# A ring of eight row tiles for the joint decode, six of them filled during chunk compression

## The reference

```
h = x + W_out( sig(gA) * W_oA(NSA(xn)) + sig(gB) * W_oB(FoX(xn)) ),  xn = RMSNorm(x)
y = h + W_down( gelu(causal_dwconv3(RMSNorm(h) W_up)) * (RMSNorm(h) W_gate) )
```

```
logits = concat([einsum('bthd,bshd->bhts', q, k) * ATTN_SCALE + cq_t - ck ... for each segment])
pr = masked_softmax(logits, mask);  out += einsum('bhts,bshd->bthd', pr, v)
```

## Time and profile before

| | |
|---|---|
| median of 3 runs | 976.39 us (976.25 to 977.01) |
| the profiled execution's own time | 969.93 us |
| its span, first to last instruction | 967.9 us |
| mean granted TensorE clock | 0.958 |
| PE busy | 867.2 us, 90% |
| DVE, ACT, POOL busy | 531.2, 367.1, 152.2 us |
| read from memory | 187.44 MB |
| decode stage, first transpose to first transpose of merge | 364.26 to 596.29 us |

### The profile page before, as it was taken

The page is one execution under the profiler, slowest core; times in us unless marked ns, Lnnn a source line. Parts: engine busy times, 40 slices in busy tenths (PEclk is TensorE's granted clock), DMA queues, the critical chain, the costliest instruction groups (busy, mean ns, idle before and its releaser), DMA issues. The chain is left out here.

```text
span 967.9 us, 18265 instructions
## 1 busy us (share of the span) xinstructions
PE 867.2 (90%) x7225; PEld 711.8 (74%) x7225; DVE 531.2 (55%) x982; ACT 367.1 (38%) x657; POOL 152.2 (16%) x255
## 2 busy tenths in 40 slices
PE   2899538979999999999999976999979999999996
PEld 1788337778988987665665533999669989898984
DVE  5544377863343476673465524555556656566654
ACT  2232455544243433363223412434325444344430
POOL 0000303301112103323333330000001101010100
PEclk9899877999999999999999986999979999999999
DMA  6352196017422349989999997968124553465311
GB/s 210 121 166 76 32 286 233 25 52 170 175 94 88 108 156 373 382 307 380 415 419 414 375 417 213 237 166 300 43 70 153 206 182 130 133 204 184 130 43 58
DMA packets 95963, 191.82 MB, mean 198 GB/s; under 512 B 7418, under 2 KB 74778, under 8 KB 83514
## 3 DMA queue, kind: packets, MB, share of 16 engines
q1 hardware_dynamic: 80060, 87.58, 29.4%
q0 software_dynamic: 14544, 102.90, 27.3%
q10 hardware_dynamic: 1296, 0.45, 0.2%
HBM read 187.44 MB, written 7.64 MB: 202 GB/s over the span
## 5 line engine op out<-in xcount | busy, mean ns | idle before, releaser
L244 PE MATMUL banks<-tokens_turned_high,w_gates_high 128*128 128x288 f32 x320 | 96.9, 303 | 3.7 <-PEq L191 2.3
L1429 PEld LDWEIGHTS banks<-consts_base,stream_rows 128*128 128x128 f32 x672 | 74.4, 143 | 33.3 <-issue 27.3
L246 PE MATMUL banks<-tokens_turned_high,w_gates_low 128*128 128x288 f32 x320 | 96.7, 302 | 0.0
L245 PE MATMUL banks<-tokens_turned_low,w_gates_high 128*128 128x288 f32 x320 | 95.4, 298 | 0.0
L1650 ACT ACTIVATE keys_turned<-banks 128x512 f32<-128x512 f32 x94 | 55.1, 596 | 103.8 <-PE banks L1429 103.7
L1429 PE MATMUL banks<-consts_base,stream_rows 128*128 128x128 f32 x672 | 83.8, 278 | 6.9 <-DMA stream_rows<-in_state_win_k 2.2
L995 PE MATMUL banks<-chunks_turned_high,cmp_w_high 64*128 64x256 f32 (+1 forms) x512 | 76.3, 293 | 5.3 <-DVE cmp_w_low L237 2.7
L995 PE MATMUL banks<-chunks_turned_low,cmp_w_high 64*128 64x256 f32 (+1 forms) x512 | 73.1, 280 | 0.0
L995 PE MATMUL banks<-chunks_turned_high,cmp_w_low 64*128 64x256 f32 (+1 forms) x512 | 72.9, 280 | 0.0
L1631 DVE COPY keys_turned<-banks 128x512 f32<-128x512 f32 x74 | 50.4, 690 | 32.8 <-PE banks L1429 30.0
L244 PEld LDWEIGHTS banks<-tokens_turned_high,w_gates_high 128*128 128x128 f32 x320 | 62.2, 194 | 4.9 <-issue 2.7
(11 more groups left out here) (429 smaller groups left out, 2058.8 us busy)
## 6 DMA issues: line engine op xcount, KB each, us to landing
w_up_gate<-in_w_up SPq DMA_DIRECT2D x12, 1024.0 KB, 7.3
w_up_gate<-in_w_gate SPq DMA_DIRECT2D x12, 1024.0 KB, 9.8
w_down<-in_w_down SPq DMA_DIRECT2D x12, 1024.0 KB, 5.0
w_in_slot<-in_w_in SPq DMA_DIRECT2D x8, 1424.0 KB, 6.2
w_gates<-in_w_in SPq DMA_DIRECT2D x16, 512.0 KB, 5.4
cmp_w<-in_cmp_w_k SPq DMA_DIRECT2D x4, 512.0 KB, 21.2
cmp_w<-in_cmp_w_v SPq DMA_DIRECT2D x4, 512.0 KB, 11.3
stream_rows<-in_state_win_k SPq DMA_DIRECT2D x8, 256.0 KB, 8.7
```

The costliest lines, as they stand in the source:

```text
L244: nc.tensor.matmul(out, lh, rh, start=start, stop=False, **kw)
L245: nc.tensor.matmul(out, lh, rl, start=False, stop=False, **kw)
L246: return nc.tensor.matmul(out, ll, rh, start=False, stop=stop, **kw)
L1429: ins = nc.tensor.transpose(bank(t)[:, q * P:(q + 1) * P], src, ident)
```

## The change

The ring gets eight tiles, and each item waits for item n - 8. Tiles 4 and 5 are placed in the upper half of the bridge, where the raw compression weights lie during compression; POOL fetches items 4 and 5 into them once `w_low` is 8, ahead of items 0 to 3. Tiles 6 and 7 are taken where tiles 4 to 6 stood. To make room, `keys_turned` has two buffers, and a new memory of 16 KB a partition (`shared_16k`) is used in turn by one low part of the input weights with the turned sample tokens, by the low compression weights, by logits and constants of decode, and by the first up and gate weights. Several smaller tiles move into one memory (`decode_side`), over which the merge stage lays its `branch_out` tiles. The first `w_o` load waits for the last use of slot 5 in place of `nacc_taken`, and DVE's last split waits for the last use of slot 4.

```diff
@@ stage_project
-        wl = [c.sb(f"w_in_low{u}", [P, KD, ZC], F32R, ctx=ctx) for u in range(2)]
+        wl = [c.sb("w_in_low0", [P, KD, ZC], F32R, ctx=ctx), c.in_big("w_in_low1", [P, KD, ZC], F32R, 0)]
@@ stage_compress
-        w1l = c.sb("cmp_w1_low", [P, 2 * CS, CH], F32R, ctx=ctx)
+        w1l = c.in_big("cmp_w1_low", [P, 2 * CS, CH], F32R, 0)
...
-            for n in range(4):
-                pool.wait_ge(turned, NSTEP - 4 if n < 2 else NSTEP)
+            pool.wait_ge(w_low, 8)
+            for n in (4, 5, 0, 1, 2, 3):
+                if n < 4:
+                    pool.wait_ge(turned, NSTEP - 4 if n < 2 else NSTEP)
                 gather_decode_rows(c, n)
@@
-DEC_RING = 7
+DEC_RING = 8
@@ stage_decode
-    kbuf = {step: n % 3 for n, step in enumerate(keys)}
+    kbuf = {step: n % 2 for n, step in enumerate(keys)}
+    last_in = lambda r: [item for n, item in enumerate(ring) if n % R == r][-1]
...
-        kT = [c.at(f"keys_turned{u}", [P, 4, 4 * P], F32, u * 4 * 4 * 4 * P) for u in range(3)]
-        FL = c.sb("fox_logits", [P, (SLOTS + 1) * P], ctx=ctx)
-        L = {br: c.sb(f"{br}_logits", [P, W[br]], ctx=ctx) for br in W}
-        pT = [c.at(f"nsa_probs_turned{u}", [P, 4 * P], F32, (12 + u) * 4 * 4 * P) for u in range(2)]
+        kT = [c.at(f"keys_turned{u}", [P, 4, 4 * P], F32, u * 4 * 4 * 4 * P) for u in range(2)]
...
+        FL = place("fox_logits", [P, (SLOTS + 1) * P])
+        L = {"win": place("win_logits", [P, W["win"]]), "cmp": place("cmp_logits", [P, W["cmp"]]), "sel": c.sb("sel_logits", [P, W["sel"]], ctx=ctx)}
+        pT = [c.sb(f"nsa_probs_turned{u}", [P, 4 * P], ctx=ctx) for u in range(2)]
...
-            sp.wait_ge(nacc_taken, 8)
+            release(sp, ring.index(last_in(5)))
             load_wo(c, sp, c.wo, c.wo_in, 0)
...
-            for n in range(4, len(ring)):
+            for n in range(6, len(ring)):
...
-                    if n >= 3:
-                        eng.wait_ge(products, done[keys[n - 3]])
+                    if n >= 2:
+                        eng.wait_ge(products, done[keys[n - 2]])
...
             dve.wait_ge(c.merge_high, 1)
+            release(dve, ring.index(last_in(4)))
             split_low(nc, c.gates_low[:, :, :, :], c.gates[:, :, :, :], c.gates_high[:, :, :, :]).then_inc(c.merge_low, 1)
@@ stage_merge
-        oh = c.sb("branch_out_high", [P, 2, 4, NTOK], F32R, ctx=ctx)
-        ol = c.sb("branch_out_low", [P, 2, 4, NTOK], F32R, ctx=ctx)
+        oh, ol = c.branch_high, c.branch_low
@@ build
+        c.big_at = -(-nc.sbuf_base // 32) * 32
+        c.sb("shared_16k", [P, 4 * KD * P])
...
+            c.stream += [c.at(f"stream_rows{n}", [P, CS * KVW], F32, 4 * (n - 2) * CS * KVW) for n in (4, 5)]
...
-            c.stream += [c.sb(f"stream_rows{n}", [P, CS * KVW], ctx=mid) for n in range(4, DEC_RING)]
+            c.stream += [c.sb(f"stream_rows{n}", [P, CS * KVW], ctx=mid) for n in (6, 7)]
```

More of the change, by code:

```diff
@@ L199, in at, with in_big @@
         return self.nc.alloc_sbuf_tensor_at(name, shape, dt, offset=self.bridge_at + offset)
+    def in_big(self, name, shape, dt, offset):
+        return self.nc.alloc_sbuf_tensor_at(name, shape, dt, offset=self.big_at + offset)
     def constants(self, group, ctx, loaded):
@@ L204, in constants, with constants_in @@
         t = self.sb(f"consts_{group}", [P, src.shape[1]], ctx=ctx)
+        at = 0
+        for name in CONST_GROUPS[group]:
+            self.views[name] = t[:, at:at + self.widths[name]]
+            at += self.widths[name]
+        return lambda e: e.dma_start(t[:, :], src).then_inc(loaded, 16)
+    def constants_in(self, group, place, loaded):
+        src = self.d[f"consts_{group}"]
+        t = place(f"consts_{group}", [P, src.shape[1]])
         at = 0
@@ L1319, in stage_decode, with place @@
     last_turn = lambda step: first[step] + {"keys": 3}.get(step[0], 0) + 1
-    kbuf = {step: n % 3 for n, step in enumerate(keys)}
+    kbuf = {step: n % 2 for n, step in enumerate(keys)}
+    last_in = lambda r: [item for n, item in enumerate(ring) if n % R == r][-1]
     with c.stage() as ctx:
         tiles = [x[:, :].rearrange("p (a e) -> p a e", a=4) for x in c.stream]
-        kT = [c.at(f"keys_turned{u}", [P, 4, 4 * P], F32, u * 4 * 4 * 4 * P) for u in range(3)]
-        FL = c.sb("fox_logits", [P, (SLOTS + 1) * P], ctx=ctx)
-        L = {br: c.sb(f"{br}_logits", [P, W[br]], ctx=ctx) for br in W}
-        pT = [c.at(f"nsa_probs_turned{u}", [P, 4 * P], F32, (12 + u) * 4 * 4 * P) for u in range(2)]
+        kT = [c.at(f"keys_turned{u}", [P, 4, 4 * P], F32, u * 4 * 4 * 4 * P) for u in range(2)]
+        big = [0]
+        def place(name, shape):
+            t = c.in_big(name, shape, F32, big[0])
+            big[0] += -(-4 * int(np.prod(shape[1:])) // 32) * 32
+            assert big[0] <= 16 * KD * P
+            return t
+        FL = place("fox_logits", [P, (SLOTS + 1) * P])
+        L = {"win": place("win_logits", [P, W["win"]]), "cmp": place("cmp_logits", [P, W["cmp"]]), "sel": c.sb("sel_logits", [P, W["sel"]], ctx=ctx)}
+        pT = [c.sb(f"nsa_probs_turned{u}", [P, 4 * P], ctx=ctx) for u in range(2)]
         turned_probs = lambda i: pT[0][:, :] if i == 2 else pT[1][:, (0, P, 0, 2 * P)[i]:(P, 2 * P, 0, 3 * P)[i]] if i < 4 else L["sel"][:, (i - 4) * 4 * P:(i - 3) * 4 * P]
-        acc = [c.at(f"fox_slot_sums{u}", [P, FW], F32, (14 + u) * 4 * FW) for u in range(2)]
+        acc = [c.sb(f"fox_slot_sums{u}", [P, FW], ctx=ctx) for u in range(2)]
         fpT = c.sb("fox_probs_turned", [P, (SLOTS + 1) * P], ctx=ctx)
@@ L1341, in stage_decode @@
         selb = c.sb("block_mask", [P, NSELB], ctx=ctx)
-        selx = c.sb("row_mask_and_shift", [P, P], ctx=ctx)
+        selx = place("row_mask_and_shift", [P, P])
         o = c.sb("nsa_rows_out", [P, KVW], ctx=ctx)
@@ L1354, in stage_decode @@
         nsa_in, select_in = c.sem("nsa_constants_in"), c.sem("select_constants_in")
-        load_nsa, load_select = c.constants("nsa", ctx, nsa_in), c.constants("select", ctx, select_in)
+        load_nsa, load_select = c.constants_in("nsa", place, nsa_in), c.constants("select", ctx, select_in)
         turned, products = c.sem("decode_turned"), c.sem("decode_products")
@@ L2225, in __init__ @@
         self.c = c
-        self.slot = lambda u, ctx: (c.sb(f"w_up_gate{u}", [P, 2, KD, 2 * P], ctx=ctx), c.sb(f"w_down{u}", [P, 2, D], ctx=ctx))
+        self.slot = lambda u, ctx: (c.sb(f"w_up_gate{u}", [P, 2, KD, 2 * P], ctx=ctx) if u else c.in_big("w_up_gate0", [P, 2, KD, 2 * P], F32, 0),
+                                    c.sb(f"w_down{u}", [P, 2, D], ctx=ctx))
         self.w_ug, self.w_dn = [[x] for x in self.slot(0, ctx)]
@@ L2503, in build @@
         c.merge_high, c.merge_low = c.sem("merge_weights_high"), c.sem("merge_weights_low")
+        side = (("nsa_q_decode", [P, DB, NH * DS]), ("fox_q_decode", [P, 4 * 2 * P + 32]), ("nsa_k_turned", [P, 2, 3, P]),
+                ("fox_k_turned", [P, 4, 3, P]), ("cmp_k_turned", [P, ND + PCH]))
+        side_at = -(-nc.sbuf_base // 32) * 32
+        side_sizes = [4 * int(np.prod(shape[1:])) for _, shape in side]
+        c.sb("decode_side", [P, sum(side_sizes) // 4])
+        (c.qb, c.fqb, c.kT, c.fkT, c.kcT) = (nc.alloc_sbuf_tensor_at(name, shape, F32, offset=side_at + sum(side_sizes[:n]))
+                                             for n, (name, shape) in enumerate(side))
+        c.branch_high, c.branch_low = (nc.alloc_sbuf_tensor_at(f"branch_out_{x}", [P, 2, 4, NTOK], F32R, offset=side_at + n * 8 * 4 * NTOK) for n, x in enumerate(("high", "low")))
+        c.big_at = -(-nc.sbuf_base // 32) * 32
+        c.sb("shared_16k", [P, 4 * KD * P])
         c.stored, c.cmp_rows_out = c.sem("results_stored"), c.sem("cmp_rows_stored")
@@ L2512, in build @@
             c.eighth_number = c.sb("eighth_row_as_number", [P, DB], ctx=mid)
[L2513 to L2516, removed]
             c.neglf = c.sb("neg_logf", [P, 3, NH], ctx=mid)
@@ L2519, in build @@
             c.png = c.sb("prompt_branch_gates", [P, QT, 3 * NH], ctx=mid)
-            c.kcT = c.sb("cmp_k_turned", [P, ND + PCH], ctx=mid)
             c.vc = c.sb("cmp_v", [P, DB, KVW], ctx=mid)
             c.stream = [c.sb(f"stream_rows{n}", [P, CS * KVW], ctx=mid) for n in range(4)]
+            c.stream += [c.at(f"stream_rows{n}", [P, CS * KVW], F32, 4 * (n - 2) * CS * KVW) for n in (4, 5)]
             c.fox_in = c.sem("fox_constants_in")
@@ L2532, in build @@
                 with ExitStack() as early:
-                    c.xsT = c.sb("sample_turned", [P, KD, NS], ctx=early)
+                    c.xsT = c.in_big("sample_turned", [P, KD, NS], F32, 4 * KD * ZC)
                     w = [c.at(f"w_in_slot{u}", [P, KD, ZC], F32, u * 4 * KD * ZC) for u in range(2)]
```

## The result

| | median us (range), runs | ratio to before, 95% interval |
|---|---|---|
| before, beside it | 973.90 (968.81 to 977.01), 9 | |
| changed kernel | 968.05 (964.37 to 971.91), 9 | 0.9939 [0.9916, 0.9962] |
| changed, second set | 968.88, 12 | 0.9951 [0.9924, 0.9978] |
| changed, third set | 968.73, 12 | 0.9955 [0.9938, 0.9972] |

The change makes the kernel faster by 4 to 6 us (medians of the three pairs). The forecast was 4.5 us, taken from the 976.39 us of the three runs shown, which are three of the nine in the first row; the time it named, 971.9, and its lower end, 968.8, are both too high. In the sets further down 95 runs of the kernel before had medians of 973.8, 972.2 and 972.4 us.

A forecast was written before the change was run, and what follows sets the result against it. It held that the last tile's landing sets decode's end, after back-to-back transfers with one hole. 2.5 + 2.0 + 0 + 0 = 4.5 us off 976.39 gave 971.9 us, range 968.8 to 976.7.

The forecast's parts named there:

- the level: Whole kernel: the 4.5 us gain subtracted from the shown runs' median, 976.39 us, gives 971.9.
- the term for the hole: Decode, 536 to 544 us: lost transfer time between two late-requested tiles would be regained, 2.0 us.
- rival (b): Tiles fetched before decode count in full, 5.0 us, plus 2.0 for the transfer gap: 969.4 us; chance 0.08.
- (c): Decode's fetch stream gains nothing because the rate falls to 402 GB/s with eight transfers in flight: 976.4 us; chance 0.11.
- Part 1: Decode ring: with eight tiles each fetch is asked for one item earlier, one transfer gained, 2.5 us.
- Part 2: Decode near 540 us: the gap in the transfers closes and the gain reaches the last tile, 2.0 us more.
- Part 3: Before decode: six tiles fetched instead of four count nothing and cost compression nothing, 0 us.
- Part 4: Edits that pay for the memory (two key buffers, moved tiles, later waits, early `w_o`): 0 us, bound 1.3.
- Key copies that wait for products: Decode key steps: seven of 42 delayed by a 1.07 us product step would make the kernel slower.
- `w_o` comes ahead: End of decode: 0.52 MB of this load ahead of the last tiles, bound 1.3 us, taken as 0.
- The tail keeps its length: After decode's last tile: the tail hangs on that tile and its length does not change.
- the 2.5 that it gave as a sign of being wrong: Merge stage: a start less than 2.5 us earlier would show the prediction wrong.

The follow-up runs named there:

- `before_again`: The kernel before, unchanged, timed and profiled once more against itself: 974.22 us, ratio 1.0011.
- the busy tail: Eight and seven tiles, window loads by GpSimd, unread products on TensorE at the end: 965.89 and 968.91 us.
- `ring7_six_early`: Changed kernel with seven tiles in the ring for eight, six still fetched in chunk compression: 973.28 us, 0.9999 of before.
- both experiments: Changed kernel with only four tiles fetched in compression, 967.72 us; and with seven ring tiles, six fetched early, 973.28 us.
- `ring7_windows_pool`: Kernel before, ring of seven, with the window tiles' loads issued by GpSimd in ring order, not SyncE: 969.64 us, 0.9959 of before.
- `after_again`: The changed kernel, unchanged, timed and profiled once more: 968.88 us, 0.9951 of before.
- `ring8_warm`: Changed kernel with unread products on TensorE ahead of the last waits: 967.28 us, 0.9941 of before.

## Why the prediction was half right

**The step that failed is the last one of the sum, the level.** It set the profile's 969.93 us beside the median of three runs, 976.39, and took the 4.5 us from that. The nine runs beside the changed kernel have 973.90, so 2.5 of the 3.9 us by which the forecast missed (971.9 against 968.05) are the level, and 1.4 the effect, which is 5.9 in that pair. Over 107 runs of the kernel before (the 95 and `before_again`'s 12) the median is 972.9 us, with 5% under 969.9 and 5% over 977.5: the three runs stood together in the upper part, the profile at the lower edge. 972.9 - 4.5 = 968.4, and the changed kernel's 33 runs have 968.6. That the effect comes out so close is luck in part, since the term for the hole was small and the terms do not add, as below. The range was built as the effect's alone, from rival (b) to rival (c); it gave the base's own scatter no width at all.

**Part 1, 2.5 us for the eighth tile: right, perhaps a little large.** The bytes at 84 us give one tile, and the last tile stands 2.4 us apart with the windows by GpSimd, 2.0 with the busy tail. In total time it is 3.0 us with the busy tail, and only 0.8 without, where the tails differed.

**Part 2, 2.0 us for the hole: right in kind, and probably too small.** It rests on an execution with one late window item. Two of the three profiles with seven tiles and SyncE's window rows (`before_again`, `ring7_six_early`) have two, and with them the last tile ends its wait at 225.3 and 224.6 us for 222.3. "PE shows no wait on a DMA before 521" was true of only that one of the three. Moving the windows' queue gives the term by itself, 2.0 to 5.9 us in total time, with the short tail of its profile in it. The keys were asked for 3.1 us earlier in the stage (506.36 - 364.26 = 142.1, now 504.66 - 365.61 = 139.1), not the 4.0 that I had from the value step.

**Part 3, early tiles 0: right,** by both experiments. Rival (b) is refuted.

**Part 4, 0: right as far as tried.** The layout with two key buffers, at seven tiles, is at 0.9999 of before, to within 3 us. Key copies that wait for products were one of the prediction's signs of being wrong. The profile after does put two such waits down to products (1.99 us before a copy by DVE at 515.40, 2.70 by ACT at 544.35), but the one at 515.40 is no longer than the copy's wait for its transposes at the same step before, 1.99 us at 513.15, and PE waits for no key copy longer than before (0.7 us). That `w_o` comes ahead (bound 1.3 us) happened and costs nothing that can be measured.

**"The tail keeps its length": wrong, by a cause that I had not looked for.** It is 9.73 and 10.84 us in the two profiles of before, 9.97, 10.84 and 10.84 in three of after, and 8.70 in `ring7_windows_pool`, by the granted clock behind the last waits. It took nothing from the change on average that these five can show, but it is why the two terms do not simply add in the profiles: the window edit alone gets the short tail in its one profile, and the eighth tile on top of it then brought 2.4 us at the tile and 0.3 at the merge stage.

**The sum by steps.** The last tile's wait ends at 222.3 and 225.3 us before, and at 219.2, 217.7 and 218.3 after: means of 223.8 and 218.4, 5.4 us apart. `ring7_windows_pool` stands between them at 220.8: 3.0 us for the window rows and 2.4 for the tile, by single profiles. Outside the stage little changed: its start lies at 364.3 and 366.5 us before and at 365.6, 365.0 and 367.4 after, and from the merge stage's first transpose to the end it is 371.6 and 371.2 us before, and 371.3, 371.6 and 369.5 after, a mean of 0.6 us less. The 5.4 us go with the 4.4 to 5.9 us of the three ratios. The first pair of profiles alone fell short of what the prediction named: the last tile's wait 3.1 us earlier for 4.5, the merge stage 2.9 in the stage's own time and 1.5 in absolute time, which is under the 2.5 that it gave as a sign of being wrong.

## What to carry to other kernels

Where the stream of bytes sets the end, the eighth tile of this ring was worth about one transfer, whatever was fetched before the stage: count the bytes moved by the end of the stretch that the engine sets, and compare. The step from six to seven was worth 14 us, so a transfer for a tile is what it comes to only where the engine hardly stands inside the stream. Before a tile is bought with memory, look at the stream's own stragglers: here moving the window rows to the ring's queue, an edit of a few lines, brought 2.0 to 5.9 us by itself, about as much as the whole change, though one execution in twelve of it took 2163 us for a reason not found. And a median of three runs is a level with its own error; when the profile lies 0.7% beside it, the range has to hold both.

## What was not expected of the hardware

- About half of the scatter between executions goes with TensorE's granted clock: over 107 runs of the kernel before the time and the mean clock (0.949 to 0.966) have a correlation of -0.74, whose square is 0.55, and within the kernels here 0.01 of it goes with 4.2 us. The start of the decode stage lay between 364.3 and 370.4 us in the fourteen profiles; the changed kernel alone had 365.0, 365.6 and 367.4.
- After PE had stood 0.77 and 1.76 us for its last two tiles (`after_again`), the granted clock was 0.50 up to the merge stage 10.84 us later; with unread products in those gaps (`ring8_warm`) it was 0.98. Waits of 1.30 and 1.87 us in `ring7_windows_pool` were not followed by slow steps; what made the difference is open.
- The rate of loads was 411 to 419 GB/s with a ring of six, seven or eight 1.049 MB tiles, from 120 to 172 us of the stage. The Trainium skill, "HBM Reference", section "Specifications (TRN2)", has about 425 GB/s for a core that streams alone, and these traces come within 1 to 4% of it; the 358 GB/s that the prediction argued with is that page's share for two cores at work.
